# Shared keys of the second attention: one split over all partitions, and the copy in the other half by two GpSimd transfers, in a two-layer hybrid backbone on one core

## What is computed

```
h  = modulate(rms_norm(x, g_mix[l]), sh1, sc1)
... sw_q, sw_k, sw_v ... = split_in(h @ w_in[l])
o_c = window_attention(apply_rope(heads(sw_q, 8), cos, sin),
                       apply_rope(heads(sw_k, 2), cos, sin),
                       heads(sw_v, 2), kc_sw, vc_sw, sw_sink[l])
# query heads 0..3 read key head 0, query heads 4..7 read key head 1
```

## Time and profile before

| what | value |
|---|---|
| median of three runs | 1831.51 us (1829.9 to 1831.65) |
| the profiled execution's own time | 1829.78 us |
| its span, first to last instruction | 1827.9 us |
| PE busy | 1680.5 us, 92% |
| DVE busy | 765.3 us, 42% |
| ACT busy | 478.8 us, 26% |
| POOL busy | 104.9 us, 6% |
| mean granted TensorE clock | 0.98 |
| HBM read | 539.13 MB |

### The profile page before, as it was taken

One profiled execution on the slowest core, in us unless ns is written; L12 is line 12 of the kernel. 1 busy time (PEld: TensorE's weight loads), 2 busy tenths in 40 slices (PEclk: granted clock), 3 DMA queues, 4 the chain that ended last, 5 costly groups with the idle time before them and its releaser, 6 DMA issues.

```text
span 1827.9 us, 26445 instructions
## 1 busy us (share of the span) xinstructions
PE 1680.5 (92%) x10822; PEld 973.9 (53%) x10822; DVE 765.3 (42%) x1742; ACT 478.8 (26%) x1050; POOL 104.9 (6%) x147
## 2 busy tenths in 40 slices
PE   5999999999998999999998799989998997776876
PEld 3887777776664333333232498878883332222222
DVE  4455566674434233333323565577753222111111
ACT  4224455552133000000000435465441000000001
POOL 1101210000001000000000012300000000000000
PEclk9999999999999999999999899999999999999998
DMA  9533232127779999999999874336899999999996
GB/s 353 159 92 95 84 93 59 35 81 259 266 276 361 409 428 427 426 428 427 428 427 427 317 217 145 87 117 210 295 374 402 425 426 426 426 426 426 425 426 286
DMA packets 149986, 543.82 MB, mean 298 GB/s; under 512 B 10026, under 2 KB 88304, under 8 KB 124652
## 3 DMA queue, kind: packets, MB, share of 16 engines
q1 hardware_dynamic: 147056, 535.35, 74.7%
q0 software_dynamic: 2400, 6.16, 1.3%
q10 hardware_dynamic: 412, 0.64, 0.1%
HBM read 539.13 MB, written 2.98 MB: 297 GB/s over the span
## 4 chain that ended last, share of the span: by engine, by line
PE 69%; DMA 23%; DVE 3%; ACT 2%; SPq 1%; issue 1%; POOL 0%; DVEq 0%; ACTq 0%
PE bank L2238 20%; PE bank L2097 11%; PE bank L2098 10%; PE bank L2099 10%; DMA ring<-in_w_exp_down 8%; DMA ring<-in_w_exp_gate 7%; DMA ring<-in_w_exp_up 5%; DMA spare<-in_w_exp_gate 3%; PE bank L1991 2%; PE bank L2126 2%; PE bank L2150 2%; PE bank L2212 2%; PE bank L2136 2%; PE bank L2267 1%; DMA ring<-in_w_in 1%
## 5 line engine op out<-in xcount | busy, mean ns | idle before, releaser
L2238 PE MATMUL bank<-ring,XEP 128*32 128x256 f32 (+1 forms) x2384 | 386.9, 619 | 37.7 <-DMA ring<-in_w_exp_gate 20.0
L2097 PE MATMUL bank<-HH,WH 128*128 128x512 f32 (+1 forms) x800 | 286.2, 358 | 4.3 <-DVE HL L1677 3.8
L2098 PE MATMUL bank<-HL,WH 128*128 128x512 f32 (+1 forms) x800 | 275.4, 344 | 0.0
L2099 PE MATMUL bank<-HH,WL 128*128 128x512 f32 (+1 forms) x800 | 274.9, 344 | 0.0
L2238 PEld LDWEIGHTS bank<-ring,XEP 128*32 128x32 f32 (+1 forms) x2384 | 115.5, 131 | 278.9 <-issue 229.8
L1646 DVE TENSOR_TENSOR WL<-ring,WH 128x1024 fp32r<-128x1024 f32 (+1 forms) x172 | 185.6, 1081 | 140.2 <-ACT WH L1405 139.4
L1913 DVE TENSOR_TENSOR X<-X,bank 128x512 f32<-128x512 f32 x184 | 114.0, 682 | 187.6 <-PE bank L2267 99.6
L1405 ACT CAST WH<-ring 128x1024 fp32r<-128x1024 f32 (+1 forms) x172 | 158.1, 927 | 126.4 <-PE bank L2099 64.7
L2238 PE MATMUL bank<-ring,HIDT 128*32 128x256 f32 (+1 forms) x1232 | 153.7, 482 | 30.2 <-DMA ring<-in_w_exp_down 30.2
L2097 PEld LDWEIGHTS bank<-HH,WH 128*128 128x128 f32 x800 | 151.8, 190 | 50.4 <-issue 28.5
L2099 PEld LDWEIGHTS bank<-HH,WL 128*128 128x128 f32 x800 | 151.9, 190 | 18.6
(11 more groups left out here) (252 smaller groups left out, 2037.6 us busy)
## 6 DMA issues: line engine op xcount, KB each, us to landing
ring<-in_w_exp_gate SPq DMA_DIRECT2D x55, 2048.0 KB, 31.3
ring<-in_w_exp_up SPq DMA_DIRECT2D x49, 2048.0 KB, 34.0
ring<-in_w_exp_down SPq DMA_DIRECT2D x48, 2048.0 KB, 36.1
ring<-in_w_ada SPq DMA_DIRECT2D x48, 1024.0 KB, 7.5
ring<-in_w_in SPq DMA_DIRECT2D x40, 1024.0 KB, 8.2
split_slot<-in_w_exp_up SPq DMA_DIRECT2D x8, 2048.0 KB, 29.4
split_slot<-in_w_exp_down SPq DMA_DIRECT2D x8, 2048.0 KB, 34.0
ring<-in_w_in SPq DMA_DIRECT2D x28, 512.0 KB, 5.2
```

The source lines that it names most:

```text
L2097: mm(t, wh, hi[:, k, 0:b.n], start=k == 0, stop=False)
L2098: mm(t, wh, lo[:, k, 0:b.n], start=False, stop=False)
L2099: last = mm(t, wl, hi[:, k, 0:b.n], start=False, stop=k == b.kk - 1)
L2238: last = mm(out_bank[tw * g:tw * g + tw, 0:nw], stationary(k), w[:, g::G] if spread else w[:, nw * g:nw * g + nw], start=k == 0, stop=k == ...
```

## The change

The key block is split once, over all 128 partitions: one `cast` of 128 x 512 and one subtraction of 128 x 512. In `dup` the last index now tells own (0) from swapped (1). A new step `swap` stands behind `finish_low`: GpSimd waits for `qk_ready` and issues two transfers from SBUF to SBUF, each of 64 partitions x 2 parts x 512 (256 KB), which put each half's keys on the opposite partitions. PE waits for both before the "sw" scores of p = 0 and picks own or swapped by the head.

```
-                b.casts = [0, 1] if b.out == "sk" else [0]
+                b.casts = [0]
...
             P.add("finish_low", blk=b)
+            if b.out == "sk":
+                P.add("swap", blk=b)
...
+                    elif s.kind == "swap":
+                        pool.wait_ge(qk_ready, s.blk.rope)
+                        for half in range(2):
+                            here, there = slice(64 * half, 64 * half + 64), slice(64 - 64 * half, 128 - 64 * half)
+                            pool.dma_start(dup[there, :, 1, :], dup[here, :, 0, :]).then_inc(dup_swapped, 16)
...
-                            for half in range(2):
-                                last = nc.scalar.copy(dup[64 * half:64 * half + 64, 0, s.hh, 0:b.n], QT[64 * s.hh:64 * s.hh + 64, 0:b.n])
+                            last = nc.scalar.copy(dup[:, 0, 0, 0:b.n], QT[:, 0:b.n])
...
-                            for hh in range(2):
-                                own = slice(64 * hh, 64 * hh + 64)
-                                for half in range(2):
-                                    last = nc.vector.tensor_tensor(dup[64 * half:64 * half + 64, 1, hh, 0:b.n], QT[own, 0:b.n],
-                                                                   dup[own, 0, hh, 0:b.n].bitcast(f32), ALU.subtract)
+                            last = nc.vector.tensor_tensor(dup[:, 1, 0, 0:b.n], QT[:, 0:b.n], dup[:, 0, 0, 0:b.n].bitcast(f32), ALU.subtract)
...
+                        if x.br == "sw" and x.p == 0:
+                            pe.wait_ge(dup_swapped, 32 * (l + 1))
...
-                                k = KS[x.p % 2][rows, kp, k0:TOK] if x.br == "na" else dup[rows, kp, x.p // 2, k0:TOK]
+                                k = KS[x.p % 2][rows, kp, k0:TOK] if x.br == "na" else dup[rows, kp, int(x.p // 2 != x.hh), k0:TOK]
```

More of the change, by code:

```diff
@@ L1051, in hybrid_dit_kernel @@
         qk_ready = sem("qk_ready")
+        dup_swapped = sem("dup_swapped")
         bias_in = [sem(f"bias_in{i}") for i in range(2)]
```

## The result

The changed kernel took 1837.02 us, median of 6 runs (1834.57 to 1839.11); the kernel before, beside it on the same chip, 1829.81 us, median of 6 (1827.57 to 1831.65). The ratio is 1.0042, with a 95% interval from 1.0032 to 1.0051: slower by some 7.7 us, between 5.9 and 9.3 (the medians themselves differ by 7.2). The profiled execution took 1839.11 us, 1.8 of it around the span.

A forecast was written before the change was run, and what follows sets the result against it. PE bounds layer 0, DVE and ACT layer 1's attention, DMA the experts' end. Late maxima 8.3 us plus clock 1.1, on a median of 1831.5, gave 1841 us; range 1833 to 1846.

The forecast's parts named there:

- A: Layer 1: p = 3 bias fetches wait behind GpSimd's swap and SP's load; maxima 8.3 us later; 1841 us, chance 0.62.
- Savings: Layer 1: one cast saves ACT 1.9 us; DVE's subtractions fall from 2.78 to 0.7; PE's transposes come 1.2 us earlier.
- The queue behind the burst: Layer 1: GpSimd's transfers go behind SP's earlier weight loads, which keep the engines full until about 1200 us.
- rival B: Layer 1: swap and biases share the DMA engines with SP's load; maxima 2.4 us late, 1834 us; chance 0.18.
- The swap: Layer 1: its 0.52 MB add 1.6 us of transfer ahead of the biases, between 1.4 and 2.6.
- The clock: Layer 1: PE stands some 10 us and its granted clock then dips, costing 1.1 us, between 0 and 3.4.
- Layer 0: Second mask ends at 257.5 us, before its use, so 0 us lost; 3 us as the other end.
- PE's wait for the swap: Layer 1: swap lands by 1203 us, well before the first "sw" scores, so it costs nothing.
- the experts' stage: From 1400 to 1800 us the DMA engines run full, so layer 1's delay is not regained and counts one to one.
- Rival C: Layer 1: biases are there in time, DVE's saving remains, maxima 3.3 us earlier; 1828.2 us, chance 0.04.
- my own halves: Rivals' chances, some split in half, summed against a 0.2% limit: slower 0.81, within 0.16, faster 0.03.

The follow-up runs named there:

- experiment 1: Changed kernel with the swap step moved, in both layers, behind the bias fetches and masks of p = 3; 1825.77 us, ratio 0.9986 to the kernel before.
- experiment 3: Changed kernel without the two swap transfers and PE's wait for them, GpSimd still waiting for DVE's subtraction; 1834.09 us, ratio 1.0026 to the kernel before.
- experiment 4: Changed kernel with SP's weight loads in layer 1 held until the swap has landed; 1831.65 us, ratio 1.0015 to the kernel before.
- experiment 6: Changed kernel with 42 matmuls of no use ahead of PE's wait in layer 1; 1836.17 us, ratio 1.0037 to the kernel before.
- experiment 5: Changed kernel with 34 matmuls of no use ahead of PE's wait in layer 1; 1837.05 us, ratio 1.0045 to the kernel before.

## Why the prediction was right, and where it was not

It said 1841 us with 1833 to 1846 as the range, slower at 0.81; measured 1837.0, slower by 0.42%. Of the 4 us between, some 1.7 are the base: I started from 1831.5, and the kernel before took 1829.8 beside the changed one. The mechanism is that of A, the forecast, in its main line, and the runs show it: with the swap behind the biases the loss is gone (experiment 1).

- *Savings.* I had the subtraction and PE's transposes 1.2 us earlier. From the event at the head of the stretch the transposes come at 5.97 us (1192.70 - 1186.73) and not at 7.54: 1.57 us earlier. Some 0.2 of this is no saving of ACT's: in the kernel before a mask (1184.44, 1.39 us long) lies beside DVE's rotation of the keys, whose multiplication at 1185.49 takes 0.62 us in place of 0.42, and in the changed kernel that mask isn't there yet. GpSimd's first swap issue comes at 6.81 us; I had it at 6.96.
- *The queue behind the burst.* **The first term that was mis-sized, and its picture was half wrong.** I had q0 silent until q1's burst had ended. It was silent for some 3 us and then moved about half of the packets while the burst went on. Without the swap this put the mask at 14.07 us (experiment 3) where my working gives 1202.0 - 1185.39 = 16.6: 2.5 us too much for the burst. So rival B, the sharing, holds from 1199 us on. But B let the transfers start at once, which puts the mask 5.45 us after the swap's issue. It was 10.29, and A said 11.25. B was also priced too low: it left out most of the 2 us between the burst's end and the mask that A had, and with them B says about 7 us. The rule of the Trainium skill (DMA: Bandwidth & Descriptors, section "Queues, rings and completion order") that each engine alternates packet by packet agrees with the equal shares from 1199 us on, 85 packets beside 89, and not with none beside 573 in the three us from 1194.
- *The swap.* I took 1.6 us between 1.4 and 2.6; it was 3.03, above my upper bound, with the delay by its issues in it. In experiment 4, where it ran alone, q0 moved 0.19 MB in one us at a share of 101.1%, and q1's weight loads move 1.14 MB in three us at 101.7%, 0.38 in one: the swap goes at half the rate, and 0.52 MB at 0.19 MB a us are 2.7 us. The Trainium skill (SBUF — State Buffer, section on the DMA port swizzle) states this for transfers that reach 64 partitions, and here the trace agrees with the rate. Whether the 64 partitions make it, or that these transfers also read from SBUF, no run here tells. The 2.4 us estimated from that page were the better term. I had no row of such a transfer and put my trust in the rate of another kind.
- *The two errors partly cancel.* The mask is at 17.10 us, my working had 18.2, and the maxima ended 7.28 us late (from 1185.39 to 1198.98 before is 13.59 us, from 1186.73 to 1207.60 after 20.87) and not 8.3. Of the 1.45 us that the sum had too much (9.4 against 7.95), 1.0 is here.
- *The clock.* **The second term that was mis-sized.** I took 1.1 us, it is 0.25 (experiment 6), although the granted clock did fall as forecast, to half and then 0.70. I had priced the stretch at the low clock as if PE set the pace in most of it. PE was waited for only at the scores, and only in the changed kernel did the low clock last until then; in experiments 3, 4 and 5 it cost nothing.
- *The masks beside DVE.* Not in the sum at all: 0.42 of the 0.67 us in the tail, since a late mask now meets DVE's addition.
- *Layer 0.* Nothing, as forecast, but not for the reason given. I had the second mask ended at 257.5 us, before its use. It began at 260.99, as GpSimd waited 5.78 and then 4.71 us for landings where I had put 3.2, and DVE waited 2.08 us for it. It cost nothing because PE had other work. That is luck in the argument.
- *PE's wait for the swap, the experts' stage.* Nothing, as forecast: PE waits nowhere for the swap in the trace, and the stretch carries the whole loss within its interval of 5.9 to 9.3 us, so nothing clear of noise was given back later.
- *Rival C* named the right condition: biases there in time, and the saving remains. I had 3.3 us for it; experiment 1 shows 2.45 in the stretch and 0.14% in the runs.
- *The chances.* By my own halves "within" sums to 0.17 and "faster" to 0.02, not 0.16 and 0.03.

## What to carry to other kernels

In a queue that runs in order, a step that waits for late data holds up every prefetch written behind it, and on the least busy engine (6% here) this is easy to miss: ask of each added wait what is queued behind it and how many us early that was. Here the small transfers that were started behind a large burst paid for the burst: 5.66 us of the loss went when it was held back. The same change that lost 7.95 us with the swap ahead of the prefetches gained 2.45 with the swap behind them. Put the step after what is due sooner, before giving up the idea.

## What the runs showed of the hardware that I had not expected

- GpSimd's queue did not wait for SP's burst to drain, and did not share from the start: no packet in 1194 to 1197, 2 in the next us, then about half. Whether the silence belongs to GpSimd's way of issuing or to the engines' queues no run here tells; in experiment 4, without a burst, the first packets came between 1.0 and 1.3 us after the issue began.
- A swap between the halves of the partitions moved 0.19 MB a us with the engines fully busy, half of the 0.38 of SP's weight loads.
- A mask on GpSimd and an addition on DVE that overlap ended together: 0.68 or 0.69 in place of 0.15 us on DVE, 1.08 to 1.20 in place of 0.72 on GpSimd, in four kernels. The Trainium skill (SBUF — State Buffer, section "Who interferes with whom") has a DVE instruction with two SBUF inputs and a GpSimd instruction that reads SBUF exclude each other, for the whole of one. The rows agree on both sides: the mask is long where it starts within a low part, and the addition ends with the mask. The kernel before has such an overlap at another place, a mask of 1.39 us at 1184.44 that starts within a low part, so it isn't the change that brings it. It was not tried by itself.
- Behind a pause of 1.91 us in PE the granted clock was 0.63 in the next stretch, after 0.94 (experiment 5). What the fall cost depended on what waited for PE while it lasted: 0.24 us in the changed kernel, nothing in experiments 3, 4 and 5.
